# A mixer and mixture-of-experts layer on one core: the first expert's down matrix fetched in the output stage, and spare multiplications in TensorE's waits

## The reference

```python
h = h + hybrid_mixer(rms_norm(h), ...) @ w_out          # 1040 rows of 1024
xn = rms_norm(h)                                        # 1024 tokens are kept
# route: a softmax over 4 groups picks one, a softmax over its 8 experts picks two
# expert_block, for the rows of each of the 32 experts:
hid = silu(xb @ w_gate[e]) * (xb @ w_up[e])             # 1024 -> 512
y = hid @ w_down[e]                                     # 512 -> 1024
out = rms_norm(h + sum over a token's two experts of weight * y)
```

## Time and profile before

| | |
|---|---|
| median of 3 runs | 1344.77 us (1341.58 to 1347.65) |
| profiled execution, its own time | 1344.94 us |
| its span | 1343.1 us |
| TensorE busy in the span | 1292.4 us, 96% |
| mean granted clock | 0.988 |

### The profile page before, as it was taken

The page is one execution under the profiler, slowest core; times in us unless marked ns, Lnnn a source line. Parts: engine busy times, 40 slices in busy tenths (PEclk is TensorE's granted clock), DMA queues, the critical chain, the costliest instruction groups (busy, mean ns, idle before and its releaser), DMA issues. The chain is left out here.

```text
span 1343.1 us, 19059 instructions
## 1 busy us (share of the span) xinstructions
PE 1292.4 (96%) x7544; PEld 1131.8 (84%) x7544; DVE 904.8 (67%) x1060; ACT 721.5 (54%) x919; POOL 179.4 (13%) x144
## 2 busy tenths in 40 slices
PE   6999999999999999989998999999999999999997
PEld 5989998999899999967887788888888888888874
DVE  6753556355645464534237889889898989888967
ACT  6351235123512351424223778888787887887844
POOL 0020112011201120430001111111111111111100
PEclk9999999999999999999996999999999999999999
DMA  7100010000000000305514999999999999999978
GB/s 206 48 16 19 30 32 32 17 32 32 32 17 32 32 32 1 126 0 225 199 63 165 369 373 377 390 390 390 393 394 386 387 384 367 382 393 375 381 284 343
DMA packets 38047, 273.56 MB, mean 204 GB/s; under 512 B 8147, under 2 KB 8403, under 8 KB 25700
## 3 DMA queue, kind: packets, MB, share of 16 engines
q1 hardware_dynamic: 28340, 251.67, 49.4%
q0 software_dynamic: 9216, 16.80, 3.3%
q10 hardware_dynamic: 432, 4.27, 0.8%
HBM read 260.11 MB, written 29.36 MB: 216 GB/s over the span
## 5 line engine op out<-in xcount | busy, mean ns | idle before, releaser
L950 DVE TENSOR_TENSOR w_lo<-w_raw,w_hi 128x2048 fp32r<-128x2048 f32 x192 | 433.0, 2286 | 33.2 <-ACT w_hi L731 32.6
L731 ACT ACTIVATE w_hi<-w_raw 128x2048 fp32r<-128x2048 f32 x192 | 360.6, 1915 | 90.6 <-DMA w_raw<-in_w_up 59.2
L1285 PE MATMUL bank<-xn_hi,p_hi 128*128 128x364 f32 (+1 forms) x672 | 229.2, 341 | 2.1 <-DVE p_lo L1736 2.1
L1287 PE MATMUL bank<-xn_hi,p_lo 128*128 128x364 f32 (+1 forms) x672 | 216.8, 323 | 0.0
L1286 PE MATMUL bank<-xn_lo,p_hi 128*128 128x364 f32 (+1 forms) x672 | 216.6, 322 | 0.0
L585 PE MATMUL bank<-w_hi,xgT_hi 128*128 128x512 f32 x512 | 206.2, 403 | 2.9 <-DVE xgT_lo L1008 2.9
L587 PE MATMUL bank<-w_hi,xgT_lo 128*128 128x512 f32 x512 | 201.2, 393 | 0.0
L586 PE MATMUL bank<-w_lo,xgT_hi 128*128 128x512 f32 x512 | 200.6, 392 | 0.0
L1285 PEld LDWEIGHTS bank<-xn_hi,p_hi 128*128 128x128 f32 x672 | 127.8, 190 | 2.9 <-DVE p_lo L1736 2.5
L1286 PEld LDWEIGHTS bank<-xn_lo,p_hi 128*128 128x128 f32 x672 | 128.0, 190 | 0.3
L1287 PEld LDWEIGHTS bank<-xn_hi,p_lo 128*128 128x128 f32 x672 | 127.6, 190 | 0.0
(11 more groups left out here) (253 smaller groups left out, 2023.1 us busy)
## 6 DMA issues: line engine op xcount, KB each, us to landing
w_raw<-in_w_down SPq DMA_DIRECT2D x32, 2048.0 KB, 10.4
w_raw<-in_w_gate SPq DMA_DIRECT2D x31, 2048.0 KB, 11.0
w_raw<-in_w_up SPq DMA_DIRECT2D x31, 2048.0 KB, 10.0
p_raw<-in_w_tiles SPq DMA_DIRECT2D x28, 512.0 KB, 3.3
arena<-y_rows SPq DMA_DIRECT2D x8, 1024.0 KB, 14.1
arena<-in_tokens SPq DMA_DIRECT2D x10, 416.0 KB
w_out_raw<-in_w_out SPq DMA_DIRECT2D x4, 1024.0 KB, 8.8
arena<-in_tokens SPq DMA_DIRECT2D x8, 512.0 KB, 4.4
```

The lines of the kernel that those rows point to most:

```text
L731: nc.scalar.activation(w_hi[m][:, half], wraw[m][:, half], ACT.Copy).then_inc(hi_done[m], 1)
L950: nc.vector.tensor_tensor(w_lo[m][:, half], wraw[m][:, half], w_hi[m][:, half].bitcast(F32), ALU.subtract).then_inc(lo_done[m], 1)
L1285: nc.tensor.matmul(out[:, 0:n], p_hi[slot][:, k, :], hi, start=(k == 0), stop=False)
L1287: m = nc.tensor.matmul(out[:, 0:n], p_lo[slot][:, k, :], hi, start=False, stop=(k == KD - 1))
```

## The change

Two things are changed.

- The down matrix of expert 0 is fetched by SP in the output stage, behind the store of block 5, once `yT` has been read for the last time. For that the routing's scratch moves: `slot1h`, `ids`, `wparts` and the weights lie in the zone of `w_out_hi`, whose products are over by then, and the other scratch lies behind the raw buffer. The two waits ahead of the old place of the fetch go with it.
- `keep_warm(n)` issues n multiplications of 128x128 by 512 columns of `w_out_hi` into bank 7, which nobody reads before something else is written there. They wait for nothing. Nine stand ahead of the L562 product, five behind it, nine ahead of `turn(0)` and five behind it.

```diff
-        zr = Zone(zy.end - 8320, zy.end)
-        slot1h = place("slot1h", zr.at, 2 * NT, 128)
+        zt = Zone(NF - KD * L, NF)
+        slot1h = place("slot1h", zt.at, 2 * NT, 128)
...
+        zr = Zone(zy.end - 8320 + WU, zy.end - 8320 + 7680)
...
                 sp.dma_start(h_dram[rows, :], h_sb[t % 3]).then_inc(h_stored, 16)
+                if t == 5:
+                    sp.wait_ge(y_hi_done, 5)
+                    sp.wait_ge(y_lo_done, 5)
+                    load_unit(sp, 0, 2)
                 sp.wait_ge(x2_done, t + 1)
...
             refill(1, 0, 1)
-            sp.wait_ge(gathered[1], 16)
-            sp.wait_ge(tables, 2)
-            load_unit(sp, 0, 2)
             sp.dma_start(fw, fin_w).then_inc(fw_loaded, 16)
...
+            def keep_warm(n):
+                for _ in range(n):
+                    nc.tensor.matmul(bank[7][:, :], w_out_hi[:, 6, 0:128], w_out_hi[:, 7, 0:512], start=True, stop=True)
+
+            keep_warm(9)
             for n in range(2 * NT):          # slot1h by ids, L562
...
             m.then_inc(r_pe, 1)
+            keep_warm(5)
             pe.wait_ge(r_dve, ROW_VALS)      # then slot1h by wparts, L567
...
+            keep_warm(9)
             turn(0, 0, 16)
+            keep_warm(5)
             gate_up(0, 0, 0, range(KD))
```

More of the change, by code:

```diff
@@ L307, in layer_kernel @@
         lo_done = [sem(f"w_lo_done{i}") for i in range(3)]
-        zr = Zone(zy.end - 8320, zy.end)
-        slot1h = place("slot1h", zr.at, 2 * NT, 128)
[L312 to L319, removed]
+        zt = Zone(NF - KD * L, NF)
+        slot1h = place("slot1h", zt.at, 2 * NT, 128)
+        zt.take(2 * NT, 128)
+        ids = place("ids", zt.at, 2 * NT, 2 * E)
+        zt.take(2 * NT, 2, E)
+        wparts = place("wparts", zt.at, 2 * NT, 2 * E)
+        zt.take(2 * NT, 2, E)
+        weight_hi = place("weight_hi", zt.at, 2 * NT)
+        zt.take(2 * NT)
+        weight_lo = zt.take(2 * NT)
+        zr = Zone(zy.end - 8320 + WU, zy.end - 8320 + 7680)
         ids_v, wparts_v = (v.rearrange("p a (k e) -> p a k e", k=2) for v in (ids, wparts))
```

## The result

| | before | after |
|---|---|---|
| median of 20 runs each, one chip | 1344.75 us | 1351.38 us (1344.25 to 1355.85) |
| ratio | | 1.0043, 95% interval 1.0032 to 1.0055 |
| profiled execution, its own time | 1344.94 us | 1352.25 us |
| its span | 1343.1 us | 1350.4 us |
| mean granted clock | 0.988 | 0.986 |

The kernel is slower by 0.43%, where I had forecast 0.36% faster; the measured time lies 7 us above the top of my range.

A forecast was written before the change was run, and what follows sets the result against it. TensorE was taken to set the pace, transfers close behind, with time to win only ahead of its full stretch: 4.6 us by the first down product (steps 1 to 5) plus 0.4 (step 6), 1344.9 - 5.0 = 1339.9 us; range 1336.8 to 1344.0.

The forecast's parts named there:

- Step 4: Gate matrix of expert 1, issued 1.3 us earlier, lands at 734.7; second gate product starts 3.2 us earlier.
- Step 5: Up matrix of expert 1 lands at 742.1, ScalarE's 3.23 us wait goes, first down product starts 4.6 us earlier.
- Steps 1 to 3: Routing: small product ends 1.3 us earlier; first gate product starts at 727.8, takes 5.6 not 7.60, ends 3.8 earlier.
- The fourth rival: Routing: clock already low at 714.2, spare multiplications stand in the way, gate starts 5.9 us late; 1349.0 us, chance 0.07.
- The earlier fetch itself costs nothing: Output stage: SP's fetch of expert 0's down matrix, its waits and its 0.3 us issue delay nothing; cost 0.
- The first rival: Gate matrix of expert 1 comes no earlier after its issue (10.4 us); sum 4.1 us, 1340.8 us, chance 0.15.
- Step 6: Up matrix of expert 2: with 2 MB less in the queue, 0.4 us more won (bounds 0 and 0.8).
- Transfers as the true bound: Expert stage: transfers set the pace and TensorE merely keeps up; 6.6 us won, 1338.3 us, chance 0.15.

The follow-up runs named there:

- 28 left out: Changed kernel with 28 multiplications removed from TensorE's never-reached code for overflowing experts, so the last stage's code lies about where it was before; 1343.96 us, 0.9998 of before.
- both ends moved on: Changed kernel with 98 never-executed multiplications at the start of TensorE's program, moving both ends of the jump by one piece of code; 1344.31 us, 1.0006 of before.
- the three executions in which it never fell: Traces of: kernel before plus 28 spare multiplications (1350.97 us); changed kernel plus 28 never-executed ones (1350.84); 28 left out with expert 2's gather later (1342.60).
- early fetch alone: Changed kernel without its 28 spare multiplications, keeping only the earlier fetch of expert 0's down matrix; 1342.19 us, 0.9979 of before.
- the two other kernels without the fetch: Kernel before with 28 never-executed multiplications in TensorE's overflow code (1352.17 us), and kernel before with the 28 spare multiplications executed (1350.97 us).
- 28 more: Changed kernel with 28 more multiplications in TensorE's never-reached code for overflowing experts; 1350.84 us, 1.0050 of before.

## Why the prediction was wrong

The step that failed is the sentence behind the sum: "From there on TensorE is full, and nothing that it does is shorter", with "That the last stage shifts with it". I had costed the 28 multiplications by their execution, and not by their place in TensorE's code. They moved both ends of the jump over the unexecuted body to other places in their pieces of code, TensorE stood 6.05 us at the start of the last stage and ran one block at the lower clock. By the medians that is worth 7.4 us (the changed kernel against the one with 28 left out; 7.1 against the one with both ends moved on; by the tables' ratios 6.1 and 5.0), more than all that I had added up, and no rival of mine had it. The signs were on the page of before: a jump, a queue of code, a last stage that begins with no wait at all, and transfers at over 1.0 beside it.

Without this loss the forecast would still have been too good: 28 left out took 1343.96 us, 0.75 below before by the medians and by the ratio nothing, where I had 5.0. The terms that were too large are those of steps 4 and 5.

Point by point:

- *Steps 1 to 3*, the gate product's end 3.8 us earlier. Right where the clock holds: 3.9 to 4.0 in the three executions in which it never fell, with 2.21 us for the small product, and 3.3 with 28 left out. In the profiled execution of the change the clock was low before the first spare multiplication, and the small product starts later (13.6 us behind the last router product, not 11.9), the transposes too; the gate product, at full clock, then ends 34.2 us behind that router product, 2.0 later than before.
- *The fourth rival* (chance 0.07) had just this path: nine multiplications that end at 718.1 (the next group starts at 718.04), a small product that ends at 721.7 (the next group starts at 721.31). Its 5.9 us at the gate's start measured 4.0, since the clock came back from 730. That its 1349.0 us is the figure nearest to the time measured is luck: the delay was made up by the end of the expert stage, and the loss came from elsewhere.
- *The earlier fetch itself costs nothing*: right. The matrix lands 8.3 us after its issue at 674.44, and SP's next command goes out 8.75 us behind the store of block 5, as before.
- *Step 4*, the gate matrix 9.5 us after its issue. Wrong: 10.1 to 11.1 in the kernels with the early fetch, although nothing large stands behind it in the queue, and 10.4 to 10.7 in those without it. The first rival was right, and the term 0.6 to 1.6 us too small; TensorE's wait is 3.0 to 3.8 us where the clock holds, not 2.1, and the second gate product at best 2.3 us earlier, not 3.2.
- *Step 5*, the up matrix. Its mechanism is right: ScalarE has no wait for it in any kernel with the early fetch (3.23 us before). Its sum is not: the first down product starts at best 2.1 us earlier, counted from the last router product, and 0.6 with early fetch alone, where I had 4.6. From the first hidden turn to the second it takes 19.57 us before, 18.8 and 19.2 in the two other kernels without the fetch, and 17.7 to 18.1 with it, so 0.7 to 1.9 less.
- *The early fetch as a whole* gains 2.5 us by the medians (0.9979), the one part of the change that is measurably faster than before. That rests on one set of 12 runs; with one gather later, on another chip, the same fetch gives 0.9998 (0.9981 to 1.0015).
- *Step 6* can't be told apart from the spread.
- *Transfers as the true bound* would have shown in the early fetch alone, as 5.3 us or more; it gave 2.5, so it falls.

By its ratio to before the early fetch alone is the best of these kernels. That the spare multiplications add anything beside it, with the code in place, no run shows.

Left open: the exact boundary (it lies between .64 and .82), why the piece of code moves earlier with 28 more (one trace), why the gate matrix is slow, and why the expert stage itself is up to 4 us late in some executions.

## What to carry to other kernels

An instruction has a price beyond its execution: it moves all code behind it. Where a kernel jumps over a long unexecuted body ahead of a stage without slack, look for a wait on "issue" and for the code queue's pieces beside it, and before believing any small gain or loss make the control that adds or removes the same number of never-executed instructions. And a faster engine ahead of a late transfer gains little: when TensorE's clock was held up, it waited 3.0 to 3.7 us for the next matrix, kept 1.0 to 2.3 of the 3.3 to 4.0 us won, and lost the clock there.

## What the runs showed of the hardware that was not expected

- 28 multiplications that are never executed cost 7.5 us, and 98 more at the start of the program take such a cost away again.
- A piece of code is ready for TensorE 4.2 to 4.4 us after it moves, and moves some 3 us later in thirteen traces in which reads of 1 MB are under way than in the two in which they are held (1.3 to 1.6 in one more).
- The granted clock falls at other times in executions of nearly the same code up to there: at 716.9 us before and back from 733, from 713 to 730 after, from about 711 to 734 with early fetch alone, from 712 to 715 with 28 left out, and not at all from 713 to 743 in three others. A gain that hangs on the clock in one stretch is there in some executions and not in others: among the 20 runs of the changed kernel the ten with a mean clock of 0.991 or more have a median of 1348.8 us, the others 1352.5.
